# Two projection jobs of the second layer moved in between the turns of the normed rows

## What is computed

```
h   = rms_norm(x)
q, k, v, qi, ki, wi = split(h @ w_in_odd)   # 1024 | 256 | 256 | 512 | 64 | 8 columns
q, k, qi, ki = rope(each)
score = sum over 8 index heads of relu(qi . ki) * wi, causal
sel   = top_k(score)                        # 128 of the prompt's keys, 256 of a sample's 1032
o     = softmax attention over the selected rows, 16 heads on 4 key/value heads
x     = x + o @ w_out_odd ; then x + hier_moe(rms_norm(x)) ; final rms_norm
```

## Time and profile before

| | us |
|---|---|
| median of 3 runs | 1367.37 (1367.0 to 1368.4) |
| time of the profiled execution | 1364.1 |
| its span | 1362.3 |
| TensorE busy | 1249.3 (92%) |
| VectorE busy | 685.0 (50%) |
| ScalarE busy | 303.7 (22%) |
| GpSimd (POOL) busy | 246.2 (18%) |

### The profile page before, as it was taken

One profiled execution on the slowest core, in us unless ns is written; L12 is line 12 of the kernel. 1 busy time (PEld: TensorE's weight loads), 2 busy tenths in 40 slices (PEclk: granted clock), 3 DMA queues, 4 the chain that ended last, 5 costly groups with the idle time before them and its releaser, 6 DMA issues. The chain is left out here.

```text
span 1362.3 us, 27020 instructions
## 1 busy us (share of the span) xinstructions
PE 1249.3 (92%) x10571; PEld 703.6 (52%) x10572; DVE 685.0 (50%) x1764; ACT 303.7 (22%) x783; POOL 246.2 (18%) x537
## 2 busy tenths in 40 slices
PE   7999999989869999999699999999999599999990
PEld 4444446654446654556544444566545366555550
DVE  2139964452454543232547897776314644442325
ACT  2121134422200000011213213666502001010012
POOL 1010057001031111200201564000010312112002
PEclk9999999999979999999699999999999799999995
DMA  9343449973479999998811122333432899999966
GB/s 304 131 158 124 158 166 325 339 275 135 156 267 391 423 418 423 424 401 348 257 42 63 35 104 83 126 125 126 156 153 98 308 387 422 419 424 423 425 261 213
DMA packets 88558, 341.05 MB, mean 250 GB/s; under 512 B 26803, under 2 KB 34067, under 8 KB 74466
## 3 DMA queue, kind: packets, MB, share of 16 engines
q1 hardware_dynamic: 67466, 289.49, 55.1%
q0 software_dynamic: 11616, 37.56, 7.6%
q10 hardware_dynamic: 9344, 12.20, 2.5%
HBM read 309.09 MB, written 30.47 MB: 249 GB/s over the span
## 5 line engine op out<-in xcount | busy, mean ns | idle before, releaser
L1332 PE MATMUL banks<-arena 128*32 128x128 f32 (+1 forms) x4736 | 345.0, 330 | 13.2 <-issue 7.7
L1332 PEld LDWEIGHTS banks<-arena 128*32 128x32 f32 (+1 forms) x4736 | 240.4, 125 | 128.1 <-issue 37.6
L1918 DVE TENSOR_TENSOR arena<-arena,banks 128x256 f32<-128x256 f32 (+5 forms) x86 | 41.0, 479 | 371.8 <-PE banks L1332 257.4
L1352 PE MATMUL banks<-arena 128*32 128x256 f32 (+1 forms) x1184 | 172.6, 491 | 1.6 <-ACT arena L1812 1.6
L863 POOL DMA_INDIRECT arena<-hn_scratch,arena x94 | 90.5, 962 | 360.4 <-DVE arena L1918 319.4
L996 PE MATMUL banks<-arena 128*128 128x512 f32 x320 | 143.3, 602 | 0.6 <-DMA arena<-in_wstream 0.6
L1024 PE MATMUL banks<-arena 128*128 128x512 f32 x256 | 116.5, 599 | 0.0
L1239 PE MATMUL banks<-arena 128*128 128x512 f32 x256 | 113.5, 599 | 1.4 <-issue 0.8
L1918 DVE TENSOR_TENSOR arena<-arena 128x512 f32<-128x512 f32 (+12 forms) x218 | 88.5, 424 | 34.9 <-ACT arena L1663 18.2
L1352 PEld LDWEIGHTS banks<-arena 128*32 128x32 f32 (+1 forms) x1184 | 59.4, 123 | 89.8 <-issue 78.0
L996 PEld LDWEIGHTS banks<-arena 128*128 128x128 f32 x320 | 60.3, 193 | 70.7 <-issue 70.3
(11 more groups left out here) (303 smaller groups left out, 1364.5 us busy)
## 6 DMA issues: line engine op xcount, KB each, us to landing
arena<-in_wstream SPq DMA_DIRECT2D x109, 2048.0 KB, 8.7
arena<-in_fox_kt SPq DMA_DIRECT2D x64, 256.0 KB, 4.4
arena<-in_fox_v SPq DMA_DIRECT2D x64, 256.0 KB, 4.2
arena<-in_dsa_page SPq DMA_DIRECT2D x64, 256.0 KB, 4.1
expert_rows<-arena ACTq DMA_DIRECT2D x76, 128.0 KB, 8.9
expert_rows<-arena POOLq DMA_DIRECT2D x1, 6656.0 KB, 19.7
hn_scratch<-arena POOLq DMA_DIRECT2D x8, 512.0 KB, 3.5
expert_rows<-arena ACTq DMA_DIRECT2D x68, 32.0 KB
```

Of the source, the lines that this page charges most:

```text
L1332: last = mm(g3(bank(b, 0, 4 * n, n * j, n * j + n), 4), x[:, c, :], g3(w[:, c, :], 4)[:, :, n * j:n * j + n], start=(c == 0), stop=(c == D ...
L1352: last = mm(bank(3, 0, 8 * n, n * q, n * q + n), ht2[g % 2][:, n * c:n * c + n], w[:, c, 8 * n * q:8 * n * q + 8 * n], start=(c == 0), sto ...
L1918: return v.tensor_tensor(out, x, y, op)
```

## The change

Jobs 0 and 1 become tiles 0 and 1 of the index queries, tile 4 becomes job 2, tiles 2 and 3 stay jobs 3 and 4 (`QUERY_TILES`). On TensorE job 0 is issued behind the tail product of tile 0 and job 1 behind that of tile 1, with no companions; the turns of tiles 2, 3 and 4 and the tails of tiles 1 to 4 come after them in turn. `tail_mm1` is still raised after the fifth tail. Jobs 2 to 19 take the companions of places 0 to 71, and places 72 to 79 come after job 19. ScalarE follows: it still copies the five tails first, then evicts jobs 0 and 1 with no companions, and goes on as TensorE does. VectorE's `rope_i` waits for the job that its tile now has.

```diff
     FRONT_TILES = (4, 0, 1, 2, 3)
+    QUERY_TILES = (0, 1, 4, 2, 3)
+    AHEAD = 2
 
     def odd_job(job):
 
-        return 3 - job // 5, job % 5 if 5 <= job < 10 else FRONT_TILES[job % 5]
+        if job < 5:
+            return 3, QUERY_TILES[job]
+        return 3 - job // 5, job % 5 if job < 10 else FRONT_TILES[job % 5]
...
         def project_odd(beside):
 
-            turn_h(2, 0)
-            for t, c0, c1 in TILES:
...
-            last.then_inc(S("tail_mm1"), 1)
-            for job in range(20):
+            def product(job, companions):
                 b, (t, c0, c1) = odd_job(job)[0], TILES[odd_job(job)[1]]
...
-                    if c in (1, 3, 5):
-                        beside(4 * job + c // 2)
+                    if c in (1, 3, 5) and companions:
+                        beside(4 * (job - AHEAD) + c // 2)
                 last.then_inc(S("proj_mm1"), 1)
-                beside(4 * job + 3)
+                if companions:
+                    beside(4 * (job - AHEAD) + 3)
+
+            turn_h(2, 0)
+            for t, c0, c1 in TILES:
+                if t + 1 < NT:
+                    turn_h(2, t + 1)
+                if t == 0:
+                    pe.wait_ge(S("c_late"), 32)
+                pe.wait_ge(S("xt2"), upto("xt2", t + 1))
+                for c in range(DC):
+                    last = mm(bank(2, TAIL[1] * t, TAIL[1] * (t + 1), 0, rows(t)), xt[:, c, c0:c1], wtail[1][:, c, :],
+                              start=(c == 0), stop=(c == DC - 1))
+                if t < AHEAD:
+                    product(t, False)
+            last.then_inc(S("tail_mm1"), 1)
+            for job in range(AHEAD, 20):
+                product(job, True)
+            for at_ in range(4 * (20 - AHEAD), 80):
+                beside(at_)
...
-                for c in range(3):
-                    beside(4 * job + c)
+                for c in range(3 if job >= AHEAD else 0):
+                    beside(4 * (job - AHEAD) + c)
                 act.wait_ge(S("proj_mm1"), upto("proj_mm1", job + 1))
...
-                beside(4 * job + 3)
+                if job >= AHEAD:
+                    beside(4 * (job - AHEAD) + 3)
+            for at_ in range(4 * (20 - AHEAD), 80):
+                beside(at_)
...
         def rope_i(x):
             t = FRONT_TILES[x]
-            dve.wait_ge(S("proj_ev1"), upto("proj_ev1", x + 1))
+            dve.wait_ge(S("proj_ev1"), upto("proj_ev1", QUERY_TILES.index(t) + 1))
             rotate_heads(A1[0:rows(t), t, :], 8, t, "i_roped", x + 4)
```

More of the change, by code:

```diff
@@ L1001, in project_odd @@
         def project_odd(beside):
-            turn_h(2, 0)
-            for t, c0, c1 in TILES:
-                if t + 1 < NT:
-                    turn_h(2, t + 1)
-                if t == 0:
-                    pe.wait_ge(S("c_late"), 32)
-                pe.wait_ge(S("xt2"), upto("xt2", t + 1))
-                for c in range(DC):
-                    last = mm(bank(2, TAIL[1] * t, TAIL[1] * (t + 1), 0, rows(t)), xt[:, c, c0:c1], wtail[1][:, c, :],
-                              start=(c == 0), stop=(c == DC - 1))
-            last.then_inc(S("tail_mm1"), 1)
-            for job in range(20):
+            def product(job, companions):
                 b, (t, c0, c1) = odd_job(job)[0], TILES[odd_job(job)[1]]
```

## The result

The changed kernel takes 1383.37 us (median of 4 runs, 1382.75 to 1386.64), beside 1367.88 us for the kernel before on the same chip: a ratio of 1.0116 [1.0097, 1.0134], 15.5 us slower. On a second chip the pair stood at 1377.01 and 1363.21 us, 1.0088 [1.0056, 1.0121], 13.8 us slower. That the second chip's 1377.01 us is next to the forecast is no support for it: the kernel before is 4.7 us faster there too.

The account below looks back on a forecast made before the run. TensorE, busy 92%, was taken as the bound, with VectorE deciding the attention's start. 11.8 + 1.4 - 6.4 = 6.8, plus 3.0 for the clock, made 9.8 us slower: 1373.9 profiled, 1377.2 median; range 1371.5 to 1382.

Parts of the forecast that it names:

- the tails end later: Front on TensorE: two jobs of 14.06 us, less 2.3 from an earlier clock rise, put the tails' end 11.8 us later.
- the new wait: TensorE behind the tails waits about 1.9 us for ScalarE's copies and one eviction; net 1.4 us more.
- the last index pair: End of VectorE's index feed: tails 11.8 plus net wait 1.4 start VectorE's long stretch 13.2 us later.
- from VectorE's end to the second scores: Attention start: VectorE's 2.69 us slack and the gap before TensorE's second scores absorb delay, leaving those scores 6.4 us later.
- from there to the output projection: Attention behind the second scores: 0.4 us for exponentials and reciprocal without cover, and 3.0 for a low clock.
- the fall of the clock: TensorE's idles before the attention may drop it to 1.2 GHz; put at 3.0 us, within 1.8 to 6.5, or nothing.
- Nothing in it can be hurried: VectorE's 82.6 us of ranking and selecting before the attention holds no wait, so its length was taken as unchanged.
- It buys nothing: POOL's earlier rotations before the attention move the last turn's 1.55 us wait into an existing gap: no gain.
- the 0.6 us or less: Attention start: VectorE masks at 852.9 to 853.4 and TensorE issues the second scores at 853.45.
- Rival 2: Attention's clock stays low for 13 us: 6.8 + 6 gives 1380.2 us, or 1382.5 with late tails; chance 0.18.
- a dense product raises the clock sooner than tails and turns: Front on TensorE: full clock about 4 us into job 0, against 13.3 us of tails and turns; gives back 2.3 us.
- tails 14.1 us late: Front on TensorE: by the skill page, the dense job brings no earlier clock rise, so nothing of the two jobs is regained.

Follow-up runs that it names:

- e1: Changed kernel with jobs 0 and 1 issued behind all five tails instead of between the turns, still without companions: 1376.13 us, ratio 1.0088.
- e6: The change with one job ahead instead of two, so companions come one job later: 1365.15 us, ratio 1.0015 to the kernel before.
- e4: Changed kernel with ScalarE evicting jobs 0 and 1 before it copies the tails: 1373.74 us, ratio 1.0076 to the kernel before.
- e10: Changed kernel with POOL's query rotations 6 and 9 held until VectorE's sample selection and first query-block half are done: 1369.12 us, ratio 1.0040.
- e2: Changed kernel with six of VectorE's selection rounds (7.5 us) moved from before the attention into its jobs: 1373.92 us, ratio 1.0075.
- e3: Changed kernel with ten unread dense products added in TensorE's two idles before the attention: 1374.81 us, ratio 1.0089 to the kernel before.
- e19: Kernel before with only POOL's rotations 6 and 9 held: 1364.14 us, ratio 1.0010.
- e13: Kernel before, unchanged, profiled again to see what varies by itself: 1360.73 us in a single run.
- e15: Kernel before with twelve of VectorE's selection rounds moved into the attention and nothing else: 1373.46 us, ratio 1.0065.

## Why the forecast was right in kind and too small

By the steps of its sum, with the profiled pair and, behind it, the second pair:

| step | put | measured |
|---|---|---|
| the tails end later (part of the next row) | 11.8 | 12.0, 11.9 |
| with the new wait, the last index pair | 13.2 | 13.2, 13.1 |
| VectorE's stretch longer | 0 | 2.0, 2.0 |
| from VectorE's end to the second scores | -6.8 | -5.5, -5.5 |
| from there to the output projection | 3.4 | 4.6, 2.9 |
| sum, without the first row | 9.8 | 14.3, 12.5 |

**Right:** the tails, the new wait (1.80 us where 1.9 stood), the passing of the bound to VectorE, TensorE's two idles of 6.03 and 4.14 us, the fall of the clock in them. Runs e1 and e6 bear out that the delay of the companions is the main cause, and e4 the small part of the new wait.

**The first step that failed** is "Nothing in it can be hurried", taken with "It buys nothing" for POOL's earlier rotations. The absence of waits in VectorE's stretch was read as a fixed length. The second four copies of the query block take 0.93 us in the earlier trace rows. The first four, 5 us earlier in the same timeline, and POOL beside them:

```profile
826.41 2.38 DVE L2592 COPY arena<-arena 64x128 f32<-64x128 f32 x4
...
826.62 1.41 POOL L809 TENSOR_TENSOR arena<-arena 128x256 f32<-128x256 f32 x2 [3.05 <-ACT arena L1699]
```

The same four copies at 2.38 and at 0.93 us would have told that the length depends on POOL. The step moved POOL against VectorE and was costed on POOL's own queue alone. It is 2.0 us: VectorE's stretch from the last pair is 88.18 us where 86.18 stood, and e10 takes 4.9 us off it by holding POOL.

**The second** is the 0.6 us or less put between VectorE's end and the second scores (852.9 to 853.45); it was 1.78, in both executions. ScalarE's order has the exponentials of job 0 ahead of the eviction of the late turn. Before, that order was harmless: the exponentials ended at 844.4 us and the turn came at 845.7. Once VectorE is last, TensorE waits for both in a row. It is 1.2 us.

**The third** is only a size: 3.4 us were put for the clock and the exponentials behind the second scores, and it was 4.6 in one execution and 2.9 in the other. Rival 2 had the long low stretch, the 13 us that this profile shows. It came true in the length of the low stretch. That its 1380.2 us and the two missed terms of 3.2 make 1383.4 is luck: it put 6 us for the clock, the whole of this part was 4.6 at most, and the runs' difference has 1.2 us more that no step explains.

**A reading that is not settled**, though its number came true, is that a dense product raises the clock sooner than tails and turns. The clock rose 4.2 and 3.9 us after the start of job 0 where 4 was put. But in five of the 18 executions read (e1, e2, e3, e10, e19) it rose 3.6 to 3.9 us after the turn of tile 1, ahead of any product, and in e19 the front is that of the kernel before. In the other thirteen it rose 12.5 to 13.3 us after that turn where no job stands in the front (before, e13, e15), and 7.6 to 10.1 where one does. So the forecast's 4 us fit the more frequent case, and a case that it did not have exists. The early rise helps only with jobs in the front: with two, the tails end at 27.3 to 27.5 instead of 29.5 to 30.5, while in e1 and e19 TensorE ran idle for 1.33 and 1.25 us, the clock fell again for 10.2 us, and the tails end at 19.50 and 19.35. The Trainium skill, page "TensorE: Matmul & The Clock Gate", section "Part 1: The HAM clock gate (the "warmup" mystery)", holds that neither number nor size of the matmuls matters. On that the five early rises speak for the page and the later ones against it. Its consequence here, tails 14.1 us late, is not what was measured (12.0).

Two small readings of the prediction were off and change nothing: by the same rows the clock is back at 392.4 us and not 392.2, and it fell at 651.8 and not 651.6, so that the idle before that fall was 4.9 us.

The runs' difference of 13.8 to 15.5 us is 1.2 to 1.3 us above the landmarks' 12.5 to 14.3 in both pairs. The landmarks are those of one execution each, and ahead of the front and behind the output projection executions scatter by some microseconds; where the 1.2 us lie was not followed.

## What to carry to other kernels

Work that is moved ahead on the busiest engine pushes back all that stands behind it in that queue. If another engine lives on what stands there, read how much slack that engine has at the place where the two meet next, and take only as much as the slack holds: here one job cost nothing that the runs can tell and two cost 1%. A stretch without waits is not a fixed length: compare the same instruction's duration within it, and ask which engine was beside it. And when the bound passes to another engine, look again at every order that was harmless because that engine had been early.

## What the runs showed of the hardware

VectorE's copies of 64x128 took 0.22 us each alone and up to 0.78 beside a rotation on POOL (before, after), a two-input operation of 128x520 0.76 and 1.10 (e10, after), POOL's own pair of 128x256 operations 1.41 and 2.34 (before, after); MAX8 and MATCH_REPLACE8 kept their times.

TensorE's clock came back 3.6 to 13.3 us after the start of the same turn in executions of nearly the same code (e19 and the kernel before). It fell 2 us after an idle of 1.33 us (e1) and of 1.25 (e19) and stayed low for 10 us of full work, and for 13 us after one of 4.14 (after). As an estimate from the scatter of the tails' end (27.3 to 30.5 us with two jobs ahead) and of the attention (139.4 and 141.1 us for one kernel), a term for it in a sum is good to about 2 us either way.
